# Forget-gate columns moved into a chunk of their own, high and low matmuls of the wide blocks interleaved

## The reference, cut to what matters

```python
def odd_mixer(x, w_in, fgate_b, q_norm_w, w_uq, kv_norm_w, w_ukv, w_out):
    proj = x @ w_in        # 512 q, 512 k, 512 v, 8 forget, 512 cq, 256 ckv, 32 k_rope
    qf, kf, vf, fl, cq, ckv, kr = jnp.split(proj, cuts, axis=-1)
    log_f = jax.nn.log_sigmoid(fl.astype(F32) + fgate_b)
    fcum = jnp.cumsum(log_f, axis=1).transpose(0, 2, 1)
    o_fox = block_causal_attention(heads(qf, 8), heads(kf, 8), heads(vf, 8), fcum)
    q = heads(rms_norm(cq, q_norm_w) @ w_uq, 8)            # last 32 of 96 roped
    kv = heads(rms_norm(ckv, kv_norm_w) @ w_ukv, 8)        # 64 k, 64 v a head
    k_rope = jnp.broadcast_to(rope_2(kr[:, None], pos), ...)
    k = jnp.concatenate([kv[..., :64], k_rope], axis=-1)
    o_mla = block_causal_attention(q, k, kv[..., 64:], None)
    return jnp.concatenate([o_fox, o_mla], axis=-1) @ w_out
...
def swiglu(x, w_gate, w_up, w_down):
    return (jax.nn.silu(x @ w_gate) * (x @ w_up)) @ w_down
```

## Time and profile before

| | before |
|---|---|
| median of three executions | 1221.47 us |
| profiled execution, its own time | 1221.47 us |
| its span, first to last instruction | 1220.2 us |
| TensorE matmul busy | 1207.3 us (99%) |
| VectorE busy | 877.3 us (72%) |
| ScalarE busy | 644.4 us (53%) |
| granted TensorE clock, mean | 0.999 |

### The profile page before, as it was taken

How to read it: one execution, slowest core, us unless ns; L and a number is a source line. 1 busy time by engine, 2 the same in 40 slices (tenths; PEclk the granted TensorE clock), 3 DMA queues, 4 the chain that set the end, 5 groups by cost and what they waited for, 6 DMA issues and landing times.

```text
span 1220.2 us, 17014 instructions
## 1 busy us (share of the span) xinstructions
PE 1207.3 (99%) x6885; PEld 1042.8 (85%) x6885; DVE 877.3 (72%) x1205; ACT 644.4 (53%) x818; POOL 63.2 (5%) x84
## 2 busy tenths in 40 slices
PE   9999999999999999999999999999999999999997
PEld 8998888888777888888899888888888987888886
DVE  6757889847776798874677787777467567877744
ACT  6445666634556666653575535444327674644430
POOL 0000000000000000000007410000001001000000
PEclk9999999999999999999999999999999999999999
DMA  9654555564543555565543357555526442755530
GB/s 357 239 202 173 175 190 188 193 212 172 185 137 109 187 187 184 183 213 184 185 168 106 138 176 263 183 190 193 189 89 242 135 160 79 267 186 194 182 129 35
DMA packets 32367, 218.31 MB, mean 179 GB/s; under 512 B 3728, under 2 KB 4000, under 8 KB 7456
## 3 DMA queue, kind: packets, MB, share of 16 engines
q1 hardware_dynamic: 30560, 210.92, 49.1%
q0 software_dynamic: 1728, 6.29, 1.5%
HBM read 216.13 MB, written 1.05 MB: 178 GB/s over the span
## 4 chain that ended last, share of the span: by engine, by line
PE 93%; DVE 3%; ACT 1%; DMA 1%; POOL 1%; issue 0%; SPq 0%; DVEq 0%; POOLq 0%; ACTq 0%
PE ps L907 41%; PE ps L832 21%; PE ps L835 12%; PE ps L836 3%; PE ps L842 3%; PE ps L846 3%; PE ps L843 3%; PE ps L950 1%; PE ps L923 1%; DVE t L1456 1%; PE ps L977 1%; PE ps L960 1%; DMA t<-in_wts 1%; PE ps L1029 0%; PE ps L882 0%; PE ps L1043 0%
## 5 line engine op out<-in xcount | busy, mean ns | idle before, releaser
L907 PE MATMUL ps<-t,t 128*128 128x512 f32 (+2 forms) x2280 | 539.5, 391 | 0.0
L1456 DVE TENSOR_TENSOR t<-t,t 128x2048 fp32r<-128x2048 f32 (+2 forms) x199 | 450.5, 2275 | 108.2 <-PE ps L907 91.7
L1150 ACT CAST t<-t 128x2048 fp32r<-128x2048 f32 (+2 forms) x199 | 375.2, 1895 | 218.8 <-PE ps L907 113.1
L907 PEld LDWEIGHTS ps<-t,t 128*128 128x128 f32 x2280 | 417.8, 188 | 82.4 <-issue 1.4
L832 PE MATMUL ps<-t,t 128*128 128x512 f32 x1120 | 283.5, 392 | 0.0
L832 PEld LDWEIGHTS ps<-t,t 128*128 128x128 f32 x1120 | 210.7, 188 | 41.1
L835 PEld LDWEIGHTS ps<-t,t 128*128 128x128 f32 x1280 | 174.6, 190 | 12.5
L835 PE MATMUL ps<-t,t 128*128 128x256 f32 x1280 | 178.5, 282 | 0.0
L842 PE MATMUL ps<-t,t 128*128 128x256 f32 x360 | 91.1, 285 | 0.0
L843 PE MATMUL ps<-t,t 128*128 128x256 f32 x360 | 90.2, 283 | 0.0
L1521 DVE SCALAR_TENSOR_TENSOR t<-t,t,t 128x254 f32<-128x254 f32 (+1 forms) x176 | 73.2, 478 | 10.8 <-ACT t L1167 10.8
(11 more groups left out here) (207 smaller groups left out, 870.3 us busy)
## 6 DMA issues: line engine op xcount, KB each, us to landing
t<-in_wts SPq DMA_DIRECT2D x194, 1024.0 KB, 4.9
t<-in_rows POOLq DMA_DIRECT2D x12, 512.0 KB, 4.6
t<-in_wts SPq DMA_DIRECT2D x3, 512.0 KB, 6.3
t<-in_wts SPq DMA_DIRECT2D x2, 768.0 KB, 5.0
t<-in_wts SPq DMA_DIRECT2D x2, 592.0 KB, 3.9
t<-in_x_in SPq DMA_DIRECT2D x2, 512.0 KB, 4.1
out<-t SPq DMA_DIRECT2D x4, 256.0 KB, 2.0
t<-in_cst SPq DMA_DIRECT2D x1, 448.0 KB, 12.6
```

Source lines behind the costliest of these rows:

```text
L907: ins = mm(ps[:, t_bank(stage, t, j), 0:c1 - c0], a, w[:, k, c0:c1], start=kt == 0 and part == 0, stop=kt == KTS[stage] - 1 and part == 2)
L1150: copy(wh[:, k, 0:w], wraw[:, r, 0:w]).then_inc(s_hi, 1)
L1456: tt(wl[:, k, 0:w], wraw[:, r, 0:w], wh[:, h, 0:w].bitcast(F32), ALU.subtract).then_inc(s_lo, 1)
```

## The change

1. **Plan.** The two `ckv` chunks of 4 x 296 columns become one F chunk of 8 x 128 columns, of which 40 are used (8 forget logits, 32 rope columns; the rest is zero), and one T chunk of 8 x 256 columns. The number of chunks is the same. The F chunks of the `odd` stage are now five, and the forget chunk is number 0.
2. **Forget path.** The logits and rope columns come out in F form, in 40 partitions of bank 5. ScalarE copies them to a new tile `fk` (`fkcopy`), TensorE transposes them in two small transposes (`forget` on TensorE), and VectorE reads them from there.
3. **Order.** The text `ODD` is written anew. The forget block stands right behind `cq`, `fsoft` within `ckv`, the first latents' transposes before `t6` of `ckv` instead of at its end, `fcum` after the first query block, the third latents' transposes inside the key block instead of inside `vf`. The steps of the attention are ordered anew too.
4. **Wide blocks.** In `f_block` a wide block waits for the low part of its chunk before its first matmul, and its matmuls alternate: high, low, high, low, and at the end low, low is followed by the last high one. Number, sizes and operands are the same.

```diff
-    for k in (0, 4):
-        plan.append(("ckv", "T", "odd_w_in_2", 0, [(2056, 288), (1536, 8)], 296, 4, k))
+    plan.append(("odd", "F", "odd_w_in_2", 0, [(1536, 8), (2312, 32)], 128, 8, 0))
+    t("ckv", "odd_w_in_2", 0, 2056, 256, 8, 8)
...
-@cq fills head
-@ckv t0.0 t0.1 t1.0 t1.1 t2.0 t2.1 lrms0 t3.0 t3.1 t4.0 t4.1 +h t5.0 +l +h +l t5.1 t6.0 t6.1 forget t7.0 t7.1 latent0
-lrms1 +l +h fcrows f0.0 fsoft latent1 f0.1 f1.0 f1.1 fcum +l
-@vf t0.0 kcopy0 t0.1 qcopy0 latent2 t1.0 t1.1 +h t2.0 s16 s17 t2.1 t3.0 t3.1 n16 s18 s19 krope t4.0 n17 u16 t4.1
-vfcopy t5.0 t5.1 t6.0 t6.1 +l u17 n18 +h t7.0 +l t7.1 n19 f2.0 u18 f2.1 +h +h p17 +l qcopy1 u19 f3.0 f3.1
-@uq kcopy1 t0.0 t1.0 s20 +l p19 +h s21 s22 n20 n21 n22 t2.0 t3.0 queries0 t0.1 u20 t1.1 t2.1 +h t3.1 queries1 u21 +h
-@ukv s23 t0.0 +l u22 t1.0 p21 across0.0 kvs0 t0.1 across0.1 +l t1.1
-@odd_out kvs1 n23 across0.2 t0.0 u23 t0.1 across0.3 t1.0 across1.0 t1.1 +h +l across1.1 s24 s25 across1.3 t2.0
-across1.2 +l n24 s26 n25 p23 n26 u24 +h t2.1 u25 s27 rows7 n27 t3.0 p25 u26 s28 s29 n28 u27 s30 s31 e4 n29 n30 n31 p27
-u28 +l t3.1 u29 g4 u30 p29 u31 g5 e5 p31 +h e6 e7 g6 end
+@cq fills head f0.0
+@ckv t0.0 t0.1 t1.0 forget t1.1 fkcopy lrms0 fsoft t2.0 t2.1 t3.0 +l +l t3.1 t4.0 t4.1 +h t5.0 t5.1 +h latent0 t6.0
+t6.1 t7.0 latent1 t7.1 lrms1 f1.0 qcopy0 f1.1 fcum fcrows +l f2.0 +h latent2 f2.1 kcopy0
+@vf +l t0.0 t0.1 t1.0 s16 t1.1 t2.0 n16 t2.1 s17 t3.0 t3.1 t4.0 krope +h s18 t4.1 t5.0 n17 n18 t5.1 u16 s19 u17 t6.0
+t6.1 +l +h t7.0 t7.1 n19 vfcopy f3.0 p17 +l u18 f3.1 +l u19 +h qcopy1 kcopy1 f4.0 f4.1 p19 s20 +h n20 s21
+@uq t0.0 n21 +h t1.0 t2.0 s22 t3.0 +l u20 t0.1 queries0 t1.1 +h n22 queries1 t2.1 t3.1 u21 +h
+@ukv t0.0 s23 u22 kvs0 t1.0 +l n23 p21 across0.0 t0.1 across0.1 t1.1 kvs1
+@odd_out +l across0.2 t0.0 u23 t0.1 +l across0.3 +h t1.0 across1.0 t1.1 across1.1 s24 s25 t2.0 across1.3 across1.2 +l
+n24 s26 n25 n26 u24 p23 t2.1 u25 +h s27 t3.0 n27 p25 u26 s28 u27 n28 e4 s29 s30 p27 u28 rows7 n29 t3.1 g4 e5 n30 u29
+s31 g5 n31 p29 u30 u31 g6 +l p31 e6 e7 +h end
...
             if blk == 0:
-                pe.wait_ge(*((s_hi, split_at(i)) if stage in WIDE else (s_lo, split_at(i))))
+                pe.wait_ge(s_lo, split_at(i))
                 pe.wait_ge(*f_bank_free(stage, n))
             if stage in WIDE:
                 o = ps[:, bank + blk, :]
-                for kt in range(7):
+                for kt in range(8):
                     pe.wait_ge(*x_ready(b, kt))
-                    mm(o, H[:, kt, c], XT[:, kt, :, :].rearrange("p c s -> p (c s)"), start=kt == 0, stop=False)
-                pe.wait_ge(s_lo, split_at(i))
-                for kt in range(8):
-                    mm(o[:, 0:S], L[:, kt, c], XTh[:, kt, :], start=False, stop=False)
-                ins = mm(o, H[:, 7, c], XT[:, 7, :, :].rearrange("p c s -> p (c s)"), start=False, stop=True)
+                    x = XT[:, kt, :, :].rearrange("p c s -> p (c s)")
+                    if kt < 7:
+                        mm(o, H[:, kt, c], x, start=kt == 0, stop=False)
+                    ins = mm(o[:, 0:S], L[:, kt, c], XTh[:, kt, :], start=False, stop=False)
+                ins = mm(o, H[:, 7, c], x, start=False, stop=True)
...
-            pe.wait_ge(*((s_xl, xl_at(6, 1, 1)), (s_xl, xl_at(6, 0, 0)), (s_xl, xl_at(6, 0, 1)))[k])
+            pe.wait_ge(*((s_xl, xl_at(6, 1, 1)), (s_xl, xl_at(6, 0, 0)), (s_fk, 1))[k])
...
+        def forget():
+            pe.wait_ge(s_fk, 1)
+            pe.wait_ge(s_xl, xl_at(6, 1, 0))
+            for t in range(2):
+                ins = turn(ps[:, 6, t * 40:t * 40 + 40], fk[:, tok(t)], ident[0:40, 0:40])
+            ins.then_inc(s_fgm, 1)
...
-                if x:
-                    act.wait_ge(s_fin, 2)
...
+            elif name == "fkcopy":
+                act.wait_ge(s_f, F_AT["odd", 0])
+                copy(fk[:], ps[0:40, f_bank("odd", 0), 0:S]).then_inc(s_fk, 1)
...
-                dve.wait_ge(s_t, t_end("ckv"))
-                tt(lf[:].rearrange("p (t c) -> p t c", t=2), ps[:, 0:2, 288:296],
+                v80 = ps[:, 6, 0:80].rearrange("p (t c) -> p t c", t=2)
+                dve.wait_ge(s_fgm, 1)
+                dve.own(nc.vector.tensor_copy(krt, v80[:, :, 8:40]))
+                tt(lf[:].rearrange("p (t c) -> p t c", t=2), v80[:, :, 0:8],
                    sm[:, 48:56].unsqueeze(1).to_broadcast([128, 2, 8]), ALU.add).then_inc(s_fin, 1)
-                nc.vector.tensor_copy(krt, ps[:, 0:2, 256:288]).then_inc(s_fin, 1)
```

More of the change, by code:

```diff
@@ L487, in program @@
     km = area.take([128, 2, 768])
-    fc, fc2 = early.take([8, S]), early.take([8, S])
+    fk, fc, fc2 = early.take([40, S]), early.take([8, S]), early.take([8, S])
     vm, vf = area.take([128, 2, 512]), area.take([128, 2, 512])
@@ L543, in program @@
     s_lrms, s_latm, s_lath = sem("s_latent_normed"), sem("s_latent_turned"), sem("s_latent_hi")
-    s_lat, s_fin = sem("s_latent_lo"), sem("s_forget_in")
+    s_lat, s_fk, s_fgm, s_fin = sem("s_latent_lo"), sem("s_forget_copied"), sem("s_forget_turned"), sem("s_forget_in")
     s_lf, s_fcm, s_fc = sem("s_forget_logs"), sem("s_forget_sums"), sem("s_forget_scaled")
@@ L614, in f_bank @@
         if stage == "odd":
-            return (3, 2, 3, 2)[n]
+            return (5, 3, 2, 3, 2)[n]
         if n < 2:
@@ L626, in f_bank_free @@
         if stage == "odd":
-            return ((s_lrms, 2), (s_lrms, 1), (s_qc, 1), (s_kc, 1))[n]
+            return ((s_xl, xl_at(6, 0, 1)), (s_lrms, 2), (s_lrms, 1), (s_qc, 1), (s_kc, 1))[n]
         q = int(stage[3])
@@ L664, in t_cols @@
             return [(0, 384), (384, 768)]
-        return [(0, 296 if stage == "ckv" else 512)] if stage in T_BANK or stage == "z1" else [(0, 512), (512, 1024)]
+        return [(0, 256 if stage == "ckv" else 512)] if stage in T_BANK or stage == "z1" else [(0, 512), (512, 1024)]
     def t_bank_free(stage, t, j):
@@ L1068, in latent @@
             ins.then_inc(s_latm, 1)
+        def forget():
[4 more added lines that the diff above has]
+            ins.then_inc(s_fgm, 1)
         def forget_sums():
             pe.wait_ge(s_lf, 1)
-            pe.wait_ge(s_xl, xl_at(6, 1, 0))
+            pe.wait_ge(s_fin, 1)
             mm(ps[0:8, 6, 0:S], lf[:, 0:8], UO, start=True, stop=False)
@@ L1132, in pe_program @@
                 latent(*k)
+            elif kind == "forget":
+                forget()
             elif kind == "fcum":
@@ L1348, in odd_step @@
                 is_k, m = int(name == "kcopy"), k[0]
-                n = is_k + 2 * m
+                n = 1 + is_k + 2 * m
                 act.wait_ge(s_f, F_AT["odd", n])
@@ L1438, in act_program @@
                 heads_hi(k[0] // 16, k[0] % 16)
-            elif kind in ("lrms", "latent", "fsoft", "queries", "kvs", "across", "qcopy", "kcopy", "vfcopy"):
+            elif kind in ("lrms", "fkcopy", "latent", "fsoft", "queries", "kvs", "across", "qcopy", "kcopy", "vfcopy"):
                 odd_step(*s)
@@ L1758, in odd_step @@
                 dve.wait_ge(s_fck, 16)
-                dve.wait_ge(s_fin, 2)
                 for t in range(2):
```

## The result

The changed kernel takes 1229.8 us (median of four runs, 1229.60 to 1229.84), the kernel before in the same session 1221.62 us (four runs): a ratio of 1.0066 [1.0049, 1.0084], 8.2 us more. Forecast were 1222.7 us and a range of 1216.5 to 1230.0. The range holds the time by 0.2 us, at its upper edge, and the forecast is 7.1 us off. By the 0.2% of the prediction's own numbers the change is slower, which had a chance of 0.33 against 0.42 for no change. The time would suit rival B "at a quarter" (1229.9 us), but only half of the loss is where B puts it.

The account below looks back on a forecast made before the run. TensorE, busy 99% of the span, was taken as the bound. Wide blocks -1.6, head +1.2 and attention +1.6 gave +1.2 us on 1221.47: 1222.7 us; own range 1218.8 to 1228.6, with rivals 1216.5 to 1230.

Parts of the forecast that it names:

- rival B: Wide blocks: each width change costs the present 20 ns, fully or partly; 1246 us in full, 1229.9 at a quarter; chance 0.18.
- Part 1: Alternating order in the wide blocks: a block takes 2785 ns, 10 ns less than now, -1.6 us over 160 blocks.
- Part 2: Matmuls of the odd stage: narrower ckv -0.8 us, forget block +2.88, two small transposes 0.3; sum +2.4 us of TensorE work.
- Part 3: Waits at the odd stage's head: old ones shrink, forget transposes newly wait 0.4 us; -1.2 us together.
- Part 4: Attention's new order in the odd stage: same work, new or longer waits, +1.6 us, bounds 0 and +3.
- e7: Attention step waiting on the heads' low part of p31, behind chunk 168's low split: about 0.3 us more wait.

Follow-up runs that it names:

- the kernel with the chunk runs: Kernel before with squares and log-sigmoid ahead of the weight splits, and wide chunks as 14 high, 16 low, 2 high matmuls: 1220.80 us, 0.9997.
- The two kernels with the wait of 2.2 to 2.4 us: Kernel before with squares and log-sigmoid ahead of the splits: 1223.53 us with old wide blocks, 1220.80 us with chunks as 14 high, 16 low, 2 high.

## Why the prediction was right in range and wrong in its parts

- **What bounds it**: right. TensorE stays at 99%, and every microsecond of the result is either start-to-start time of its matmuls or a wait of its own.
- **Part 1, the failed step**: "If the two prices hold in the mix, the pair costs 233 + 114 = 347 ns". The pair costs 352.5: on the average high ones 235.3, low ones 117.2. Both prices came from one place in the earlier trace rows, where a low matmul stood behind a row of eight high ones and a high one behind a row of eight low ones. The rows already held the clue that they would not add up: the 20 ns lost were "spread over the high ones that follow", that is, the change also slows high ones that have another high one ahead of them. With a change ahead of each of them, all are slow, 8.6 ns each. Forecast -1.6, measured +4.3. (The low one behind the high group, which I had read as about 110, takes 113.3 by the single starts; the 114 of the sum was near.) Rival B had the mechanism, and it had named a loss that is paid in part only; a fifth of its full price (27 of 140 ns a block) was paid, where I gave it 0.18 and priced it at all or a quarter.
- The low part's wait at the block's start, costed at nothing: right; no wait on the low split is in the list of the FFNs or of the run with the order alone.
- **Part 2**, +2.4: the forget block is 2.88 as forecast, and with the waits it makes the head's measured +1.3 beside a forecast of +1.2.
- **Part 3**, waits: right in kind and near in size. Forget transposes wait 0.38 (period of 499 ns in place of 120; forecast 0.4), first latents 0.15 (0.3), the sums nothing (0). The run with the old attention order repeats it: +1.14.
- **Part 4**, mis-sized: forecast +1.6, bounds 0 and +3, measured +2.6 (2.8 between the two runs without it and with it). Term by term, each an excess of start-to-start time: `s20` 0.72 (0.5), `u31` 0.83 (0.4), the first normed rows' transposes 0.67, of which 0.31 stood there before the change already, so 0.36 more (0.4), and 0.27 more before the later ones, `e7` nothing more (0.3), and about 0.5 before `u24` and `u27` that I had not looked for: there the new order leaves less work between a head's scores and its use. Part of each excess is that a releaser's semaphore and the first matmul behind a wait take some 0.15 us that the listed wait does not have: the list says 0.55 for `s20`, the starts 0.72.
- **Sum**: the errors have the same sign, 5.9 us in the blocks, 1.0 in the attention and 0.1 at the head. The forecast's own range (to 1228.6) missed; only the shares of the rivals brought the range to 1230. Its upper bound for the blocks, +1.6, is worked out nowhere: Part 1's own bound in that direction is +22. That 1229.8 lies inside 1230 is luck.

## What to carry to other kernels

Price a matmul's neighbourhood by the place in a run that it has there, and not by the instruction ahead of it alone: a cost that is spread over several successors grows when a new change comes before they are through (here from 20 to 47 ns a block, for eight changes instead of one). Where matmuls of 512 and 256 columns share a phase, longer runs of each were cheaper over the four orders tried here. Before a wait is moved away, follow what it releases through every in-order queue down to the last consumer, the loads on the DMA-issuing queue among them: the three waits here stood in one line behind each other, and removing the first two made TensorE meet the third, which cost more.

## What the runs showed of the hardware that was not expected

- Behind a change from 256 to 512 columns the next five 512-column matmuls start 228 to 236 ns apart instead of 226.7, 27 ns in all, of which two 256-column ones behind the change back return 7; none of it when both have 512 columns (227.0 over 640 matmuls). What in the engine does it was not measured.
- A wait of TensorE can cost more than itself. Behind waits of 1.4 us the granted clock stayed at 1.00; behind one of 2.2 us it was 0.83 over 10 us, behind one of 5.9 us 0.78 and 0.71, and the matmuls behind it took up to twice their time (scores 2.55 us instead of 1.26): 1.7 and 3.7 us on top. Behind one of 2.4 us, in the kernel with the chunk runs, it stayed at 1.00, so the length of the wait alone does not settle it.
- The two kernels with the wait of 2.2 to 2.4 us also spread widest from run to run, over 4.6 and 4.8 us, and their times go with the mean granted clock of the run. In the first, five runs of 1221.41 to 1221.67 us have 0.998 or 0.999, four of 1223.53 to 1224.12 have 0.997, and two of 1225.22 and 1226.03 have 0.996. In the second it is 0.998 or 0.999 up to 1220.80 us and 0.997 or 0.996 from 1221.55 us on. So the first kernel is about as fast as the one before where the clock holds, and not faster; what decides whether it holds was not tried.
